# Norms between the layers of a three-block network, in other order and with unread products

## The reference

```python
def rmsnorm(x, g):
    xf = x.astype(jnp.float32)
    y = xf * lax.rsqrt(jnp.mean(xf * xf, axis=-1, keepdims=True) + EPS)
    return (y * g.astype(jnp.float32)).astype(x.dtype)
...
        h = rmsnorm(x, g_pre_ffn1[l])
        x = x + 0.5 * rmsnorm(swiglu(h, w_gu1[l], w_down1[l]), g_post_ffn1[l])
        h = rmsnorm(x, g_pre_mix[l])
...
        x = x + rmsnorm(merged @ w_out[l], g_post_mix[l])
        h = rmsnorm(x, g_pre_ffn2[l])
        x = x + 0.5 * rmsnorm(swiglu(h, w_gu2[l], w_down2[l]), g_post_ffn2[l])
...
        x = x + sq_relu_mlp(rmsnorm_2(x, norm_mlp[layer]), w_mlp1[layer], w_mlp2[layer])
    return rmsnorm_2(x, final_norm)
```

## Time and profile before

| | |
|---|---|
| median of three runs | 2566.43 us (2565.8 to 2566.77) |
| the profiled execution, its time | 2565.01 us |
| its span in the profile | 2563.2 us |
| TensorE busy | 2435.6 us (95%), 11176 instructions |
| VectorE busy | 1242.6 us (48%) |
| ScalarE busy | 979.1 us (38%) |
| GpSimd busy | 249.8 us (10%) |
| mean granted TensorE clock | 0.97 of full |
| DMA | 81 GB/s over the span |

### The profile page before, as it was taken

The page is one execution under the profiler, slowest core; times in us unless marked ns, Lnnn a source line. Parts: engine busy times, 40 slices in busy tenths (PEclk is TensorE's granted clock), DMA queues, the critical chain, the costliest instruction groups (busy, mean ns, idle before and its releaser), DMA issues.

```text
span 2563.2 us, 28444 instructions
## 1 busy us (share of the span) xinstructions
PE 2435.6 (95%) x11176; PEld 1941.0 (76%) x11176; DVE 1242.6 (48%) x2010; ACT 979.1 (38%) x1621; POOL 249.8 (10%) x180
## 2 busy tenths in 40 slices
PE   8999998999897998999998889999998879999998
PEld 6888877777775887888886667888886657888886
DVE  5533336789453436433436745424434755542433
ACT  4333223455344334322223554313324765431331
POOL 0101101322020101100102300000001220000000
PEclk9999998999998998999998989999999988999998
DMA  4323232211220231323323113222321102332221
GB/s 146 94 91 103 89 101 85 66 50 50 67 76 27 91 103 59 106 80 109 99 82 102 33 46 107 99 97 92 99 80 35 44 23 67 104 98 94 92 98 66
DMA packets 66902, 208.37 MB, mean 81 GB/s; under 512 B 7440, under 2 KB 16144, under 8 KB 66512
## 3 DMA queue, kind: packets, MB, share of 16 engines
q1 hardware_dynamic: 66768, 206.55, 25.6%
HBM read 204.42 MB, written 2.10 MB: 81 GB/s over the span
## 4 chain that ended last, share of the span: by engine, by line
PE 73%; issue 13%; DVE 5%; POOL 4%; ACT 4%; DMA 1%; POOLq 0%; SPq 0%; DVEq 0%; ACTq 0%
PE bank L1628 23%; PE bank L1630 22%; PE bank L1632 22%; POOL ftmps L2590 2%; POOL qk L2596 2%; PE bank L1747 1%; DVE wlo L2158 1%; ACT whi L1868 1%; PE bank L1685 1%; PE bank L1738 1%; DMA wraw<-in_stream 1%; PE bank L1800 1%; PE bank L1694 1%; DVE ssb L2169 1%; DVE hlo L2164 0%
## 5 line engine op out<-in xcount | busy, mean ns | idle before, releaser
L2158 DVE TENSOR_TENSOR wlo<-wraw,whi 128x1024 fp32r<-128x1024 f32 (+4 forms) x438 | 495.0, 1132 | 553.7 <-ACT whi L1868 549.5
L1628 PE MATMUL bank<-hhi,whi 128*128 128x512 f32 x1744 | 698.3, 400 | 14.1 <-issue 5.1
L1630 PE MATMUL bank<-hlo,whi 128*128 128x512 f32 x1744 | 685.8, 393 | 2.1 <-DVE hlo L2164 2.1
L1632 PE MATMUL bank<-hhi,wlo 128*128 128x512 f32 x1744 | 686.3, 393 | 1.0 <-DVE wlo L2158 0.7
L1868 ACT ACTIVATE whi<-wraw 128x1024 fp32r<-128x1024 f32 (+4 forms) x438 | 410.1, 937 | 518.2 <-PE bank L1632 463.0
L1628 PEld LDWEIGHTS bank<-hhi,whi 128*128 128x128 f32 x1744 | 331.4, 190 | 88.3 <-issue 18.4
L1632 PEld LDWEIGHTS bank<-hhi,wlo 128*128 128x128 f32 x1744 | 330.6, 190 | 74.9 <-DVE wlo L2158 3.7
L1630 PEld LDWEIGHTS bank<-hlo,whi 128*128 128x128 f32 x1744 | 331.4, 190 | 70.0 <-DVE hlo L2164 4.2
L1630 PE MATMUL bank<-mlo,whi 128*128 128x512 f32 x576 | 227.6, 395 | 0.2 <-DVE mlo L2416 0.2
L1628 PE MATMUL bank<-mhi,whi 128*128 128x512 f32 x576 | 227.6, 395 | 0.0
L1632 PE MATMUL bank<-mhi,wlo 128*128 128x512 f32 x576 | 227.5, 395 | 0.0
(11 more groups left out here) (380 smaller groups left out, 3167.0 us busy)
## 6 DMA issues: line engine op xcount, KB each, us to landing
wraw<-in_stream SPq DMA_DIRECT2D x343, 512.0 KB, 3.5
wraw<-in_stream SPq DMA_DIRECT2D x40, 192.0 KB, 2.4
wraw<-in_stream SPq DMA_DIRECT2D x22, 256.0 KB, 2.6
wraw<-in_stream SPq DMA_DIRECT2D x8, 320.0 KB, 3.0
xa<-in_x SPq DMA_DIRECT2D x8, 256.0 KB, 5.5
out<-ya SPq DMA_DIRECT2D x8, 256.0 KB, 2.6
m<-in_mask SPq DMA_DIRECT2D x1, 1024.0 KB, 4.8
wraw<-in_stream SPq DMA_DIRECT2D x8, 128.0 KB, 2.0
```

Of the source, the lines that this page charges most:

```text
L1628: pe.matmul(out, sh, xh, start=first, stop=False)
L1630: pe.matmul(out, sh, xl, start=False, stop=False)
L1632: p = pe.matmul(out, sl, xh, start=False, stop=end and last)
L2158: dve.tensor_tensor(wlo[j][:, 0:L], wraw[i][:, 0:L], whi[j][:, 0:L].bitcast(f32), SUB).then_inc(*lo.up(c))
```

## The change

It has six parts.

1. "sums" runs term by term instead of column by column: four products of `ssb`, then four of the other term. `late()` is called before the add of a tile in `ffn` (second half), in `residual` and for the mixer's output, and once more at the end of `post_norm` and `residual`, so that "sums" of norms of x has one term there.
2. `keep_busy` puts 128-column float32 products whose result nobody reads into a spare bank: 3 before the last term of "sums", 7 after "sums", and 9 after "spread", for the three y norms; the last norm has the first two.
3. VectorE does all eight adds of `post_norm`, none is on GpSimd. One more chunk is split ahead of the first "post".
4. `token_major` does "sums" of norm ("h", 1) after the fourth chunk instead of the third, and "spread" after the first chunk of the second half. The second half runs in two passes of two output tiles over the same four chunks, which stay in their buffers until the second pass. In `side_by_side` the first `R.step()` comes after the second tile instead of the first, and in `mlp` the second comes one tile later.
5. The inverse root starts with one instruction instead of two.
6. In the last stage ScalarE multiplies by the gain while the tiles still come in ("final_in"), TensorE spreads the root into two banks, VectorE multiplies six tiles from one, and GpSimd two from a copy of the other.

```diff
             b, q = MB.take(), SMR.take()
-                put("sums", self.norm, b.i, b.was)
+                put("sums", self.norm, b.i, b.was, None)
...
-    def rstd_spread(norm, n, ring=None):
+    def rstd_spread(norm, n):
...
+        b, q, spare = MB.take(), SMR.take(), TB.take()
+        put("sums", norm, b.i, (*b.was, *spare.was), spare.i)
...
+        b = MB.take()
+        put("spread", norm, b.i, b.was, ("sm", q.i), spare.i if norm[0] == "y" else None)
...
         b = rstd_spread(norm, D)
+        split_while(state["split"] + 1)
...
-                who = "x_dve" if j == 0 else "x_pool"
-                put("post_add", s, j, q.i, natural, who, (("post", (s, j)), *x_at[j]))
...
                 operand(nxt, j - 1, hfree)
+            if j < 8:
+                put("post_add", s, j, q.i, natural, (("post", (s, j)), *x_at[j]))
...
+        sx.late()
         b.free = (("post", (s, 7)),)
...
-            if n == 0:
+            if n == 1:
                 R.step()
...
             t = run(feat(keys(n), x, k_from=k_from))
+            sx.late()
             put("resid", nxt, n, t.bank, (t.end, *x_at[n]))
...
+            if nxt == 7:
+                put("final_in", n)
         if nxt < 7:
+            sx.late()
             R.begin(("h", nxt))
...
+    def token_major(tag, n, nch, w, c0, gd, some=4):
+        for t0 in range(0, 4, some):
+            ts = [Tile(G.take(), ("h", 1), 128, 0) for _ in range(some)]
+            for c in range(nch):
+                ci = opened((tag, n, c))
+                put("tm", ts, ci, plan[ci][3] * c, c == nch - 1, w, t0)
+                if t0 + some == 4:
+                    closed.add(ci)
+                if c == 0 and R.stage == 1:
+                    R.step()
+            if R.stage == 0:
                 R.step()
...
-    token_major("va", 1, 4, 512, 512, x7)
+    token_major("va", 1, 4, 512, 512, x7, 2)
...
                 ts = side_by_side(("h", s), *[(f"m{l}u0", n, 0) for n in range(3)])
+                ts.append(run(feat([(f"m{l}u0", 3, 0)], ("h", s))))
                 R.step()
...
+            def keep_busy(b, n):
+
+                for _ in range(n if b is not None else 0):
+                    pe.matmul(banks[b][:, 0:128], ones[:, :], ident[:, :], start=True, stop=True)
...
-                dve.tensor_scalar(r.bitcast(i32), v.bitcast(i32), 1, None, A.arith_shift_right).then_inc(*chain.up())
-                w.wait_ge(*chain.now())
-                dve.tensor_scalar(r.bitcast(i32), r.bitcast(i32), -1.0, 1597463007.0, MUL, ADD).then_inc(*chain.up())
+                dve.tensor_scalar(r.bitcast(i32), v.bitcast(i32), -0.5, 1597463007.0, MUL, ADD).then_inc(*chain.up())
...
+                elif k == "final_in":
+                    n, = a
+                    act.activation(ya[:, n, :], ya[:, n, :], F.Copy, scale=C("final", n)).then_inc(*final_in.up(n))
...
+                    if j < 6:
+                        w.wait_ge(*spread["h", 7])
+                        w.wait_ge(*final_in[j])
+                        dve.tensor_tensor(ya[:, j, :], ya[:, j, :], banks[b][:, :], MUL).then_inc(*final.up(j))
...
+                    pool.tensor_tensor(ya[:, j, :], ya[:, j, :], rb[:, :], MUL).then_inc(*final_pool.up(j))
```

More of the change, by code:

```diff
@@ L1207, in work_order @@
     b = rstd_spread(("h", 7), D)
-    for j in range(8):
-        put("final", j, b.i, (("spread", ("h", 7)), *x_at[j]))
+    second = G.take()
+    put("final_spread", second.i, second.was, b.col)
+    for j in (0, 1, 6, 2, 3, 7, 4, 5):
+        put("final", j, b.i)
     assert len(closed) == len(plan)
@@ L1677, in tensor @@
                 elif k == "sums":
[L1678 removed]
+                    norm, b, was, busy = a
                     terms = open_sums[norm].terms()
```

112 lines of the change are left out of this document (60 added, 52 removed).

## The result

The changed kernel takes 2552.5 us, the median of four runs (2548.9 to 2553.6), beside 2566.1 us for the kernel before (2563.0 to 2566.8). The ratio is 0.9947, with a 95% interval of 0.993 to 0.9964. That is faster by 0.36% to 0.70%, and 3.5 us slower than forecast. The profiled execution took 2553.6 us; its page begins with

What follows compares the result with a forecast made beforehand. TensorE, busy 95% of the span, was taken as the bound, so only its idle time or slow clock counted. Terms summed to -17.5 us, from 2565.0 to 2547.5; with 1.4 for the median, 2549 us, range 2544 to 2560.

Steps and rivals of the forecast that it cites:

- Part 1 and 2: Chain of the three y norms: shorter sums and root, clock held by unread products; 3.1, 2.3 and 2.1, together -7.5 us.
- rival (a): Unread products don't hold the clock, or in half the places, and stand in the way; some 4 us each, 2557; chance 0.17.
- Part 3: VectorE adds at the y norms: a tile costs VectorE 2.5 us instead of 3.01, so TensorE's 2.7 us becomes the bound.
- Part 4: Values' stage: reordered products end it at 436.6 instead of 445.86, with a new 2.7 us wait for the root; -5.6 us.
- Second and third y norm behind the restart: Restart to the end of spread: 26.9 us instead of 28.89 (-2.0), and 29.0 instead of 31.40 (-2.4).
- The residual tiles: After the mixers: running sum lengthens the VectorE chain, TensorE waits; +3.3 us after the even (bounds 0, +5), +0.8 after the odd.
- Rival (b): The residual tiles cost nothing because TensorE has buffers enough; about 2545 us; chance 0.12.
- The norm between: Norm between the two mixers' stretches: sums with one term saves 0.9 us.
- The end: Last norm and output: first multiplication 2.6 us earlier, last store issued at about 2557.2 instead of 2560.2; -2.9 us.

Runs made afterwards that it cites:

- split_behind_root: The changed kernel with the split of the third chunk of the values' second half behind the root of norm (h, 1) on VectorE: 2548.2 us.
- gpsimd_adds: The changed kernel with the y norms' additions back on GpSimd, tile 0 on VectorE as before: 2560.6 us.
- before_unread: The kernel before with the unread products alone added, its own order of sums kept: 2569.3 us, ratio 1.001.
- no_unread: The changed kernel without its unread products, at the y norms and at the end: 2557.6 us.
- last_sum_behind: The changed kernel with the running sum of a y norm's last tile again behind that tile's addition on VectorE: 2554.9 us.
- values_as_before: The changed kernel with the values' stage in its old order, four tiles side by side in both halves: 2553.1 us.
- residual_sum_behind: The changed kernel with the running sum in the mixers' residual tiles again behind the addition, only the last ahead of sums: 2551.7 us.
- one_between: The changed kernel with one unread product instead of three between the sums of the two terms: 2551.5 us.

## Why the prediction came out as it did

**Part 1 and 2, -7.5.** Measured +0.2, -2.3 and +1.2, so -0.9, and this is the step that failed. Three sentences of it were wrong. "Behind the last square, which ends at 379.84 + 0.63": I left the square where it stood, although the moved running sum stands between it and the product; it ends 0.6 us later behind the last product. "The three fit into the wait for the square (1.66 us idle)": the row says that this wait was for the running sum, which stands ahead of it; behind the running sum's products only 0.3 us are left, and in split_behind_root the second half of sums starts 0.46 us behind the square's end, at 382.02. With both, and the clock held, the first and third norm give 2.1 and 1.0 (9.87 and 10.20 us in split_behind_root) instead of 3.1 and 2.1. At the second norm the figure was met. And "I take it that the clock holds": it held at one norm of three in this execution, and in the five traces with the same norms at two of five first ones, five of five second ones and three of five third ones. That is rival (a), with its mechanism as described (seven outlast the root by 0.8, forecast 0.9) and 2.3 us a place by measurement (12.14 and 12.47 against 9.87 and 10.20) instead of the 4 that were reckoned. The nine are not in the way, since `hhi` comes later too.

**Part 3.** Right: 2.53 us an operand, forecast 2.5; TensorE is the bound behind the restart (22.2 us for the 96 products with their start). What I had not seen is that the rest hangs on it: gpsimd_adds puts its worth at 8 us (5.3 of them in the values' stage, whose gain the forecast booked under part 4), before_unread shows the unread products losing without it.

**Part 4, -5.6.** Measured -6.5. The restart came at 391.2 instead of 387.3, 3.9 later; with that shift the fetch stood where it was reckoned (410.99 against 406.9 + 3.9), the chunk landed 3.5 us behind its issue (4.3 reckoned), and the wait for the root was 1.7 to 1.9 us instead of 2.7. The wait ahead of the next stage is 1.00 (1.2). Split_behind_root shows cause and price.

**Second and third y norm behind the restart.** -2.0 and -2.0; forecast -2.0 and -2.4. The terms named for the third make 28.7 us, not the 29.0 that was put down; it took 29.4.

**The residual tiles, +3.3 and +0.8.** Measured +1.9 and +0.4. The chain was right: additions 4.68 us apart, waits on TensorE for the third chunk of the next layer, the clock falling in them. The term was too big: turning the order back gives 3.1 and not 4.5. The waits grew by about 1.5 (2.92 + 0.53 + 0.34 against 1.81 + 0.53), where I had 2.5, and low clock took the rest. After the odd mixer the order's worth can be read only at equal clocks: from its output product to the last product 386.2 us without it and with 7 us of low clock at its start; 387.8 with it and as much low clock, in no_unread and in last_sum_behind alike; so 1.6 where 2.0 was reckoned. Rival (b), that it costs nothing, is out.

**The norm between, -0.9.** Measured -0.9.

**The end, -2.9.** Measured -2.4. The rows answer:

```profile
2536.68 0.40 PE L1656 MATMUL bank<-mhi,wlo 128*128 128x512 f32 x1
...
2543.06 3.68 DVE L2595 TENSOR_TENSOR ya<-ya,bank 128x512 f32<-128x512 f32 x6 [1.25 <-PE bank L1724]
...
2543.78 5.23 SPq L1619 DMA_DIRECT2D out<-ya  x8
...
2544.63 2.67 POOL L2647 TENSOR_TENSOR ya<-ya,rb 128x512 f32<-128x512 f32 x2 [400.08 <-ACT rb L1927]
```

The first multiplication stands 6.38 us behind the last product, before 8.99: -2.6 as reckoned. The two GpSimd multiplications take 2.67 us together, unhindered, and end at 2547.3, as reckoned; but the eight stores take 5.23 us to issue, 5.02 before, so their end doesn't come forward by more than the multiplications do.

**What no term had.** +0.6 at the start; -1.1 in the stages behind the values; +1.6 in the odd mixer, where the clock fell in a stretch that has the same instructions as before (below). The stages whose code is unchanged move by 1 to 2 us either way from one execution to the next. The working had no such term, while its range did: rival (a) at 2557 and the forecast lie on both sides of 2552.5.

**What was luck.** The profiled execution was forecast at 2547.5 and took 2553.6, a miss of 6.1 us. The median missed by 3.5 only, because the forecast put it 1.4 above the profiled execution and it came out 1.1 below.

## What to carry to other kernels

When an instruction is moved ahead of another on a queue, follow the one it now stands in front of down to the next engine: here the sum that TensorE wanted early pushed the square that it wanted next. A filler that is meant to keep the clock must be counted at the low clock too, and kept short in front of what is on the path, since here it worked in one execution and not in the next. And before a faster start is counted as a gain, look at what the stage behind it waits for: without VectorE's additions the time won at the norm was waited away 18 us later, with the clock lost into the bargain.

## What the runs showed of the hardware

The same instructions had the clock fall in one execution and not in another. The first norm of the changed kernel, values_as_before, residual_sum_behind, split_behind_root and gpsimd_adds is one code: 12.14, 12.29, 10.67, 9.87 and 9.87 us, with 7, 7, 3, 0 and 0 us of low clock. The Trainium skill, "TensorE: Matmul & The Clock Gate", section "What's actually happening", says that what the gate looks at runs free of the kernel's start, and that the same kernel therefore differs from run to run; the five figures agree with it, and no run here shows the cause.

Unread products gave the clock back sooner where they hadn't kept it: behind f1 it was low for 7 us in the changed kernel (to 389.0, while they ran) and for 10 in no_unread (to 393.3, behind the restart at 390.5). Before the change it was 17 (to 398.2), so the larger part of that difference came with the rest of the change.

The clock also fell where TensorE never stood idle. In the odd mixer, behind 24 records of one-column products (from 1918.2 to 1920.8), the changed kernel and then the kernel before, all engines (busy time and instructions of PE, PEld, DVE, ACT, POOL; clock; DMA):

```profile
1916.00:1921.50 5.50, 5.50 (x38) 4.67 (x37) 0.89 (x6) 0.96 (x3) 0.00 (x0) 1.00 0.06 18
1921.50:1925.00 3.50, 3.50 (x10) 2.24 (x9) 1.46 (x9) 0.00 (x0) 0.00 (x0) 0.51 0.00 0
```

```profile
1927.00:1932.50 5.50, 5.50 (x38) 4.67 (x37) 0.84 (x5) 1.01 (x3) 0.00 (x0) 1.00 0.06 18
1932.50:1936.00 3.50, 3.50 (x17) 2.60 (x16) 1.97 (x11) 0.31 (x1) 0.00 (x0) 1.00 0.02 5
```

Busy all the time by the trace, the same instructions, and half the clock behind them in the one case: ten products in 3.5 us against seventeen, which is the 1.6 us of the table. It fell there in ten of the eleven traces of the changed kernel and its variants and in none of the three of the one before and its variants. In two of the ten, split_behind_root and one_between, the low clock ended earlier farther on in the mixer, and this stage took no longer than before. Why it goes with the kernel, and not by chance, is open; no run was made for it.
